# A double buffer for the exponents of an attention loop, turned in place, with the keys permuted as they are written

## The chip, the cores and the metric

The kernel runs on one core of a Trainium2 chip. The metric is the device time of one execution in microseconds. The kernel is written by hand for each engine: TensorE (PE) multiplies, VectorE (DVE) and ScalarE (ACT) work on its results, SyncE (SP) issues most DMAs and GpSimd (POOL) some. Engines wait for each other by semaphores that the code names. A matrix product in float32 stands in the trace as two instructions.

## The reference

Two layers of a mixed backbone over 256 context tokens and 1024 latent tokens. The change lies in the attention of each layer alone. The latent tokens attend to 512 cached keys and their own 1024, the context tokens to their own 256:

```python
s = jnp.einsum('bqhd,bkhd->bhqk', qi, k).astype(jnp.float32) * scale
p = jax.nn.softmax(s, axis=-1).astype(v.dtype)
return jnp.einsum('bhqk,bkhd->bqhd', p, v)
...
out = jnp.concatenate([attn_out, conv_out, cmlp_out], axis=-1) @ p['w_out']
```

After the projection each layer has an expert-choice feed-forward of 16 experts, which takes the larger part of the time.

## The kernel before

**Items.** Attention is cut into 18 items per layer (ITEMS, NI = 18). An item is one tile of 128 queries and a pair of heads ("slot" 0 and 1). Items 0 and 9 are the context ones (both query tiles, 256 keys each); the other 16 have 1536 keys, as 12 chunks of 128. The keys have no values of their own yet: probabilities are multiplied by the compressed context (CKVT), and value_heads expands the result afterwards.

**One item.** PE writes the scores of slot 0 to PSUM banks 0 to 2 and of slot 1 to banks 3 to 5 (scores, L1083, and the rotary part for both slots, rotary_scores, L1095). DVE takes the maximum of each slot over the 1536 keys (row_max, L1881, then L1885). ACT takes the exponents of a slot (exponents, L1539) into Pr[slot], a buffer per slot in r2. The next product needs keys on the partitions, so the exponents are transposed in two moves. DVE turns every 32x32 block (turn_blocks, L1893) from Pr[slot] to PB[slot], which lies in slot 1 of the ring; the same instruction permutes the blocks, since both of its access patterns are 4-dimensional with runs of 32 elements. Then SP issues 16 DMAs (exchange, L531), one for each pair of a destination quarter a and a source quarter b of the partitions: each moves 32 partitions x 2 runs of 384 floats into PTr[n % 2]. When all have landed (pt_landed[n % 2]), PE multiplies with the context (times_values, L1138; L1135 for the context items), in two halves of six chunks.

**Order.** Every engine runs its items in order. PE's iteration n is: scores of slot 0 of item n, the modulation matmuls of n-2 (L1109), first half of times_values(n-2), rotary scores of n, scores of slot 1, the transpose of the modulation, second half of times_values(n-2). DVE's is: bias_modulation(n-2), divide_out(n-3) (L1916), row_max of both slots, copy_modulation(n-2), turn_blocks of both slots, invert_sums (L1904). ACT's is: exponents of both slots, copy_out(n-2) (L1554). SP's is: load_ada (five DMAs: 2 MB of modulation weights, L516, and four small ones, L518) in items 0 to 7 of the first layer and 0 to 3 of the second, one of the two 2 MB units of W_OUT in each of the next two items, then the exchange. The modulation matmuls stand in PE's iterations 2 to 9 and 2 to 5. POOL sends the inverse sums through DRAM to all partitions (L717, L723), and DVE divides with them three items later.

**Waits around the change.** PB is a single buffer for both slots of one item. So turn_blocks(n) waits for pt_landed of item n-1: the DMAs must have read it. exponents(n) waits for p_turned of item n-1, and exchange(n) for p_turned of item n and, because of PTr, for o_summed of item n-2.

Of the kernel before, what the change touches and what calls it, by code (L numbers as in the profile page):

```python
# [20 lines left out]
PT = NP // P  # L21
# [24 lines left out]
ITEMS = []  # L46
# [11 lines left out]
def key_chunks(n):  # L58

    return 4 if ITEMS[n][1] is PROMPT_TILES else 12  # L60
# [48 lines left out]
def backbone(nc, x_prompt, x_sample, cache_ckv, cache_krope, c, c_ctx, w_ada, b_ada, norm1_g, norm2_g, w_in,  # L109
# [8 lines left out]
    with ExitStack() as ctx:  # L118
# [129 lines left out]
        Pr = [r2[:, 1536 * i:1536 * (i + 1)] for i in range(2)]  # L248
        PB = [ring[:, 1, 1536 * i:1536 * (i + 1)] for i in range(2)]
# [173 lines left out]
        def at(layer, per_layer, n):  # L423

            return layer * per_layer + n
# [17 lines left out]
        def _(sp):  # L443
# [21 lines left out]
            for l in range(DEPTH):  # L465
# [55 lines left out]
                def exchange(n):  # L521

                    x = key_chunks(n) * 32
                    sp.wait_ge(p_turned, at(l, 2 * NI, 2 * n + 2))
                    if n >= 2:
                        sp.wait_ge(o_summed, at(l, NI, n - 1))
                    for a in range(4):
                        for b in range(4):
                            dst = PTr[n % 2][32 * a:32 * a + 32, 0:8 * x].rearrange("p (s i x) -> p s i x", s=2, i=4)
                            src = ring[32 * b:32 * b + 32, 1, 0:3072].rearrange("p (s x) -> p s x", s=2)  # L530
                            sp.dma_start(dst[:, :, b, :], src[:, :, x * a:x * (a + 1)]).then_inc(pt_landed[n % 2], 16)  # L531

                for n in range(NI):
# [8 lines left out]
                    exchange(n)  # L542
# [12 lines left out]

                load_xd(0)
# [279 lines left out]
        def _(pe):  # L836
# [52 lines left out]
            for l in range(DEPTH):  # L889
# [230 lines left out]
                def times_values(n, chunks):  # L1120
# [8 lines left out]
                    rows = PTr[n % 2][:, 0:256 * key_chunks(n)].rearrange("p (s i x) -> p s i x", s=2, i=4)  # L1129
                    for c in chunks:  # L1130
                        if c >= key_chunks(n):
                            continue
                        moving = rows[:, :, :, 32 * c:32 * c + 32]
                        if t is PROMPT_TILES:
                            ins = pe.matmul(PS[:, 7, (c // 2) * 256:(c // 2 + 1) * 256], CKVT[:, c % 2, :], moving,  # L1135
                                            start=(c % 2 == 0), stop=(c % 2 == 1))
                        else:
                            ins = pe.matmul(PS[:, 7, 0:256], CKVT[:, PT + c, :], moving, start=(c == 0), stop=(c == 11))  # L1138
                        if c == key_chunks(n) - 1:
                            ins.then_inc(o_summed, 1)  # L1140
# [264 lines left out]
        def _(act):  # L1405
# [27 lines left out]
            for l in range(DEPTH):  # L1433
# [92 lines left out]

                def exponents(n, slot):
# [3 lines left out]
                    if n:  # L1531
                        act.wait_ge(p_turned, at(l, 2 * NI, 2 * (n - 1) + slot + 1))
                    if t is PROMPT_TILES:
                        for i in range(PT):
                            c = 2 * slot + i
                            ins = act.activation(Pr[slot][:, i * NP:(i + 1) * NP], psum(3 * slot + i, NP), ACT.Exp,
                                                 bias=nmax[:, c:c + 1], scale=SCALE, accum_out=psum_row[:, c:c + 1])
                    else:
                        ins = act.activation(Pr[slot], psum_wide(3 * slot, KEYS_S), ACT.Exp,  # L1539
# [166 lines left out]
        def _(dve):  # L1706
# [46 lines left out]
            for l in range(DEPTH):  # L1753
# [491 lines left out]
```

## Time and profile before

| | us |
|---|---|
| median of 3 runs | 2575.68 |
| lowest and highest | 2570.53, 2576.28 |
| the profiled execution | 2586.33 |
| its span from first to last instruction | 2584.6 |
| mean granted TensorE clock (share of full) | 0.957 |

Engine busy times of the profiled execution: PE 2363.8 us, DVE 746.5, ACT 509.5, POOL 277.1. The profiled execution is 10.7 us (0.4%) above the median, and 1.7 us of it lie outside its span. The chain that ended last is followed back from the last instruction: each piece of it is what released the next. "issue" in a chain is time for which the profile shows no wait. Sums of waits show how often one engine waited for another's work and how long in total.

### The profile page before, as it was taken

What the parts mean: (1) busy time and instruction counts of PE and PEld (TensorE: products, weight loads), DVE (VectorE), ACT (ScalarE), POOL (GpSimd) and SP (SyncE); (2) the same over time, 40 slices, a digit from 0 to 9 for tenths busy, and PEclk for the clock granted to TensorE, in tenths of its full rate; (3) what the DMA queues carried; (4) which work ended last, traced back from release to release, by engine and by line L of the source; (5) the groups of instructions that cost most, each with busy time, mean ns of one, the idle gap of its engine ahead of it and who ended that gap; (6) DMA issues with size and microseconds to landing.
All of it is one profiled execution on the core that took longest, in us unless ns stands there. A gap on an engine that the chain in (4) does not pass through costs nothing.

```text
span 2584.6 us, 30331 instructions
## 1 busy us (share of the span) xinstructions
PE 2363.8 (91%) x12256; PEld 1542.8 (60%) x12256; DVE 746.5 (29%) x1419; ACT 509.5 (20%) x1048; POOL 277.1 (11%) x434
## 2 busy tenths in 40 slices
PE   6999988778999899999999998877889959999996
PEld 4545545444445778878754455544444438888785
DVE  2302244444236211111142023434432371111113
ACT  3310222111234211101142002121113331101102
POOL 2000010101000121121210000210000001211211
PEclk8999999988999999999999999988899979999998
DMA  9000168755535788889940002864552248888888
GB/s 325 25 21 0 49 167 197 177 96 120 178 108 189 272 274 276 270 281 283 331 146 16 21 0 78 201 131 83 92 116 98 98 171 251 275 279 276 274 276 294
DMA packets 211770, 440.45 MB, mean 170 GB/s; under 512 B 23744, under 2 KB 71032, under 8 KB 211680
## 3 DMA queue, kind: packets, MB, share of 16 engines
q1 hardware_dynamic: 188912, 384.94, 48.0%
q0 software_dynamic: 22768, 54.29, 9.4%
q8 instruction: 59, 0.97, 0.2%
q14 instruction: 31, 0.25, 0.0%
HBM read 339.08 MB, written 47.65 MB: 150 GB/s over the span
## 4 chain that ended last, share of the span: by engine, by line
PE 68%; SPq 13%; DMA 9%; DVE 5%; issue 4%; ACT 1%; DVEq 0%; POOL 0%; POOLq 0%; ACTq 0%
SPq L531 13%; PE PS L1358 11%; PE PS L1365 11%; PE PS L1204 11%; PE PS L1390 8%; PE PS L990 8%; DMA r<-ring 6%; PE PS L944 5%; PE PS L931 5%; DVE ring L1893 2%; PE PS L1384 2%; PE PS L1044 1%; PE PS L1343 1%; PE PS L1216 1%; PE PS L898 1%
## 5 line engine op out<-in xcount | busy, mean ns | idle before, releaser
L1138 PE MATMUL PS<-r 128*128 128x256 f32 x768 | 220.9, 449 | 108.4 <-DMA r<-ring 108.4
L1358 PEld LDWEIGHTS PS<-r,ring 128*128 128x128 f32 x2048 | 281.5, 190 | 15.2 <-issue 15.2
L1204 PE MATMUL PS<-ring,mix 128*128 128x512 f32 x640 | 288.4, 598 | 1.2 <-DVE mix L1941 1.2
L1358 PE MATMUL PS<-r,ring 128*128 128x160 f32 x2048 | 283.6, 299 | 0.3 <-ACT r L1661 0.2
L1365 PE MATMUL PS<-r,ring 128*128 128x160 f32 x2048 | 283.4, 299 | 0.0
L1365 PEld LDWEIGHTS PS<-r,ring 128*128 128x128 f32 x2048 | 279.9, 190 | 0.0
L1138 PEld LDWEIGHTS PS<-r 128*128 128x128 f32 x768 | 171.4, 228 | 168.3 <-DMA r<-ring 128.8
L1390 PE MATMUL PS<-ring,r 128*128 128x512 f32 x496 | 221.1, 599 | 0.0
L990 PE MATMUL PS<-r,ring 128*128 128x512 f32 (+1 forms) x576 | 208.4, 521 | 1.6 <-ACT r L1482 1.6
L1083 PE MATMUL PS<-lat,r 128*128 128x512 f32 (+1 forms) x416 | 188.2, 587 | 10.2 <-ACT r L1539 5.4
L1204 PEld LDWEIGHTS PS<-ring,mix 128*128 128x128 f32 x640 | 116.4, 190 | 129.7 <-issue 129.7
L1539 ACT ACTIVATE r<-PS,nmax 128x1536 f32<-128x1536 f32 x64 | 98.6, 1541 | 461.6 <-DVE nmax L1885 461.6
L1893 DVE STREAM_TRANSPOSE ring<-r 128x1536 f32<-128x1536 f32 (+1 forms) x72 | 115.5, 1639 | 232.8 <-DMA r<-ring 232.1
L2153 DVE TENSOR_TENSOR r<-r,PS 128x320 f32<-128x320 f32 x64 | 31.2, 488 | 497.5 <-PE PS L1365 497.5
L990 PEld LDWEIGHTS PS<-r,ring 128*128 128x128 f32 x576 | 109.1, 190 | 100.6 <-issue 95.0
L1390 PEld LDWEIGHTS PS<-ring,r 128*128 128x128 f32 x496 | 91.7, 190 | 116.6 <-issue 116.6
L1881 DVE TENSOR_REDUCE pmax<-PS 128x1 f32<-128x1536 f32 x64 | 112.5, 1758 | 126.4 <-PE PS L1095 100.3
L944 PE MATMUL PS<-ring,r 128*128 128x512 f32 x320 | 140.0, 592 | 0.0
L1083 PEld LDWEIGHTS PS<-lat,r 128*128 128x128 f32 x416 | 75.2, 189 | 104.8 <-issue 86.8
L931 PE MATMUL PS<-ring,r 128*128 128x448 f32 x320 | 126.6, 550 | 0.0
L1672 ACT ACTIVATE r<-PS 128x320 f32<-128x320 f32 x64 | 24.5, 434 | 479.0 <-PE PS L1358 479.0
L1661 ACT ACTIVATE r<-PS,mod_all,scale_all 128x128 f32<-128x128 f32 x132 | 49.8, 456 | 277.5 <-PE PS L1343 277.5
(303 smaller groups left out, 2074.4 us busy)
## 6 DMA issues: line engine op xcount, KB each, us to landing
ring<-in_w_gate_dram SPq DMA_DIRECT2D x32, 2048.0 KB, 10.1
ring<-in_w_up_dram SPq DMA_DIRECT2D x32, 2048.0 KB, 11.6
ring<-in_w_down_dram SPq DMA_DIRECT2D x31, 2048.0 KB, 9.1
r<-ring SPq DMA_DIRECT2D x512, 96.0 KB, 4.5
ring<-in_w_ada_dram SPq DMA_DIRECT2D x15, 2048.0 KB, 10.1
x_dram<-r SPq DMA_DIRECT2D x20, 512.0 KB, 2.9
r<-x_dram SPq DMA_DIRECT2D x20, 512.0 KB, 4.2
mix<-in_w_ada_dram SPq DMA_DIRECT2D x4, 2048.0 KB, 15.0
```

The source lines that it names most:

```text
L531: sp.dma_start(dst[:, :, b, :], src[:, :, x * a:x * (a + 1)]).then_inc(pt_landed[n % 2], 16)
L931: ins = pe.matmul(psum(4 + t % 2, 448), hT[:, k, t * P:(t + 1) * P], W_IN[0][:, k, :], start=(k == 0), stop=(k == KD - 1))
L944: ins = pe.matmul(psum(t % 4, 512), hT[:, k, t * P:(t + 1) * P], W_IN[1][:, k, :], start=(k == 0), stop=(k == KD - 1))
L990: ins = pe.matmul(psum(base + j, tn), W_IN[u][:, k, c0:c0 + P], hT[:, k, t0:t0 + tn], start=(k == 0), stop=(k == KD - 1))
L1083: ins = pe.matmul(psum(3 * slot + c, w), QA[:, 2 * ITEMS[n][0] + slot, q], CKV[:, keys], start=(slot == 0), stop=(slot == 1))
L1138: ins = pe.matmul(PS[:, 7, 0:256], CKVT[:, PT + c, :], moving, start=(c == 0), stop=(c == 11))
L1204: ins = pe.matmul(psum(2 * (s % 2) + n, 512), mix[:, k, tile * P:(tile + 1) * P], W_OUT[n][:, k, :], start=(k == 0), stop=(k == KD - 1))
L1358: ins = pe.matmul(PS[:, b // 2, (b % 2) * 256:(b % 2) * 256 + SLOTS], W_G[:, k, b * P:(b + 1) * P], XST[par][:, k, :], start=(k == 0), sto ...
L1365: ins = pe.matmul(PS[:, 2 + b // 2, (b % 2) * 256:(b % 2) * 256 + SLOTS], W_U[:, k, b * P:(b + 1) * P], XST[par][:, k, :], start=(k == 0), ...
L1390: ins = pe.matmul(psum(4 + n, 512), HID[:, k, 0:CAP_S], w_down[:, k, n * 512:(n + 1) * 512], start=(k == 0), stop=(k == 3))
L1881: ins = dve.tensor_reduce(pmax[:, c:c + 1], psum_wide(3 * slot, KEYS_S), AX, ALU.max)
L1893: dve.transpose(PB[slot][:, 0:4 * x].rearrange("p (i c b) -> p c i b", i=4, b=32), Pr[slot][:, 0:4 * x].rearrange("p (c i a) -> p c i a", ...
```

## The change

It does five things, all in the attention loop.

1. Pr gets one buffer per item, for two items: the even items' exponents lie in r2[:, 0:3072], the odd ones' in ring slot 1, where PB was. PB is gone.
2. The exponents are written with the block permutation (by_chunk reads PSUM in key order, by_quarter writes quarter i of all chunks together, in runs of 32 floats).
3. The block transpose reads and writes the same contiguous range.
4. The exchange reads from Pr[n % 2]. For the 16 large items the pieces are the same as before (32 partitions x 2 runs of 384 floats). For the four context items a DMA has 4 runs of 64 floats, where it had 2 runs of 128.
5. The waits: exponents(n) waits for pt_landed of item n-2 (was p_turned of n-1); turn_blocks(n) no longer waits for pt_landed. Before the first tile of x is loaded behind the loop, SP waits for pt_landed[0], because that tile takes r2[:, 0:1024].

The context items' matmuls read their moving operand by another pattern, also in runs of 32 floats. The exchange takes its destination quarters as an argument, and the only call passes all four, in the same order as before, from SP.

```diff
-        Pr = [r2[:, 1536 * i:1536 * (i + 1)] for i in range(2)]
-        PB = [ring[:, 1, 1536 * i:1536 * (i + 1)] for i in range(2)]
+        Pr = [r2[:, 0:3072], ring[:, 1, 0:3072]]
...
-                def exchange(n):
-
-                    x = key_chunks(n) * 32
+                def exchange(n, quarters):
+
+                    groups, x = groups_of(n)
                     sp.wait_ge(p_turned, at(l, 2 * NI, 2 * n + 2))
                     if n >= 2:
                         sp.wait_ge(o_summed, at(l, NI, n - 1))
-                    for a in range(4):
+                    for a in quarters:
                         for b in range(4):
-                            dst = PTr[n % 2][32 * a:32 * a + 32, 0:8 * x].rearrange("p (s i x) -> p s i x", s=2, i=4)
-                            src = ring[32 * b:32 * b + 32, 1, 0:3072].rearrange("p (s x) -> p s x", s=2)
-                            sp.dma_start(dst[:, :, b, :], src[:, :, x * a:x * (a + 1)]).then_inc(pt_landed[n % 2], 16)
+                            dst = PTr[n % 2][32 * a:32 * a + 32, 0:4 * groups * x].rearrange("p (g x) -> p g x", g=groups)
+                            src = Pr[n % 2][32 * b:32 * b + 32, 0:4 * groups * x].rearrange("p (g x) -> p g x", g=groups)
+                            sp.dma_start(dst[:, :, x * b:x * (b + 1)], src[:, :, x * a:x * (a + 1)])\
+                                .then_inc(pt_landed[n % 2], 16)
...
+                sp.wait_ge(pt_landed[0], at(l, 256 * NI // 2, 256 * NI // 2))
                 load_xd(0)
...
                     act.wait_ge(max_ready, at(l, 2 * NI, 2 * n + slot + 1))
-                    if n:
-                        act.wait_ge(p_turned, at(l, 2 * NI, 2 * (n - 1) + slot + 1))
+                    if n >= 2:
+                        act.wait_ge(pt_landed[n % 2], at(l, 256 * NI // 2, 256 * (n // 2)))
...
-                        ins = act.activation(Pr[slot], psum_wide(3 * slot, KEYS_S), ACT.Exp,
+                        ins = act.activation(by_quarter(Pr[n % 2][:, slot * KEYS_S:(slot + 1) * KEYS_S]),
+                                             by_chunk(psum_wide(3 * slot, KEYS_S)), ACT.Exp,
...
-                    x = key_chunks(n) * 32
+                    groups, x = groups_of(n)
+                    w = 2 * groups * x
                     dve.wait_ge(exp_done, at(l, 2 * NI, 2 * n + slot + 1))
-                    if n:
-                        dve.wait_ge(pt_landed[(n - 1) % 2], at(l, 256 * NI // 2, 256 * ((n - 1) // 2 + 1)))
-                    dve.transpose(PB[slot][:, 0:4 * x].rearrange("p (i c b) -> p c i b", i=4, b=32),
-                                  Pr[slot][:, 0:4 * x].rearrange("p (c i a) -> p c i a", i=4, a=32)).then_inc(p_turned, 1)
+                    rows = Pr[n % 2][:, w * slot:w * (slot + 1)]
+                    dve.transpose(rows, rows).then_inc(p_turned, 1)
```

New functions that the diff calls:

```python
def groups_of(n):
    return (4, 64) if ITEMS[n][1] is PROMPT_TILES else (2, 384)
def by_chunk(keys):
    return keys.rearrange("p (c i a) -> p c i a", i=4, a=32)
def by_quarter(keys):
    return keys.rearrange("p (i c a) -> p c i a", i=4, a=32)
```

No instruction of the loop changes its place; its waits and buffers do. DVE in items 0 to 2 of the first layer before, from the transposes of item 0 to those of item 2 (L1881 and L1885 are the maxima, L1904 the inverse of the sums, L1954 and L1963 the modulation; "waits" names the semaphores):

```order
L1893 STREAM_TRANSPOSE ring<-r2 128x4x4x32 [waits exp_done] x2
L1904 RECIPROCAL oinv<-psum_row 128x4 [waits exp_done]
L1881 TENSOR_REDUCE pmax<-PS 128x1 [waits summed0]
L1885 TENSOR_SCALAR nmax<-pmax 128x1 [waits exp_done,dve_own]
L1881 TENSOR_REDUCE pmax<-PS 128x1 [waits summed1]
L1885 TENSOR_SCALAR nmax<-pmax 128x1 [waits exp_done,dve_own]
L1893 STREAM_TRANSPOSE ring<-r2 128x12x4x32 [waits pt_landed0,exp_done] x2
L1904 RECIPROCAL oinv<-psum_row 128x2 [waits exp_done]
L1954 TENSOR_TENSOR r1<-PS,r1 128x128 [waits ada_summed]
```

The same place now:

```order
L1905 STREAM_TRANSPOSE r2<-r2 128x512 [waits exp_done] x2
L1915 RECIPROCAL oinv<-psum_row 128x4 [waits exp_done]
L1893 TENSOR_REDUCE pmax<-PS 128x1 [waits summed0]
L1897 TENSOR_SCALAR nmax<-pmax 128x1 [waits exp_done,dve_own]
L1893 TENSOR_REDUCE pmax<-PS 128x1 [waits summed1]
L1897 TENSOR_SCALAR nmax<-pmax 128x1 [waits exp_done,dve_own]
L1905 STREAM_TRANSPOSE ring<-ring 128x1536 [waits exp_done] x2
L1915 RECIPROCAL oinv<-psum_row 128x2 [waits exp_done]
L1965 TENSOR_TENSOR r1<-PS,r1 128x128 [waits ada_summed]
```

The order is the same; the wait for pt_landed0 is gone from the transposes of item 1 (and its like from all later ones), and they work in place. ACT at the exponents of items 1 to 3 before (L1551 and L1554 are copy_out):

```order
L1539 ACTIVATE r2,psum_row<-PS,nmax 128x1536 [waits p_turned,max_ready] x4
L1551 ACTIVATE mix<-PS 128x2x256 [waits o_summed]
L1539 ACTIVATE r2,psum_row<-PS,nmax 128x1536 [waits p_turned,max_ready] x2
L1554 ACTIVATE mix<-PS 128x2x128 [waits o_summed]
L1539 ACTIVATE r2,psum_row<-PS,nmax 128x1536 [waits p_turned,max_ready] x2
```

The same place now:

```order
L1550 ACTIVATE ring,psum_row<-PS,nmax 128x12x4x32 [waits max_ready] x2
L1550 ACTIVATE r2,psum_row<-PS,nmax 128x12x4x32 [waits pt_landed0,max_ready] x2
L1563 ACTIVATE mix<-PS 128x2x256 [waits o_summed]
L1550 ACTIVATE ring,psum_row<-PS,nmax 128x12x4x32 [waits pt_landed1,max_ready] x2
L1566 ACTIVATE mix<-PS 128x2x128 [waits o_summed]
```

The exponents wait for the landing of the item two before, and write ring and r2 in turn.

## Rows read from the trace of the kernel before

**Rows 1.** The page, sections 1, 2 and 4: span, clock by slice, the chain's shares.

```profile
span 2584.6 us, 30331 instructions
...
PEclk8999999988999999999999999988899979999998
...
SPq L531 13%; PE PS L1358 11%; PE PS L1365 11%; PE PS L1204 11%; PE PS L1390 8%; PE PS L990 8%; DMA r<-ring 6%; PE PS L944 5%; PE PS L931 5%; DVE ring L1893 2%; PE PS L1384 2%; PE PS L1044 1%; PE PS L1343 1%; PE PS L1216 1%; PE PS L898 1%
```

**Rows 2.** Waits, 328 to 645 us: who <- for whom: us, times, longest.

```profile
DVE ring L1893 <- DMA r<-ring: 119.9, 17, 10.9
...
PE PS L1138 <- DMA r<-ring: 50.7, 15, 6.7
```

**Rows 3.** The chain in order of time, one item: start us, us, what.

```profile
537.75 4.84 DMA r<-ring
542.95 1.44 issue
544.39 1.75 DVE ring L1893
546.78 0.60 SPq L531
```

**Rows 4.** DVE in order of time, one item: start us, us, what [idle before].

```profile
528.03 0.12 DVE L1904 RECIPROCAL oinv<-psum_row 128x2 f32<-128x2 f32 x1
...
542.68 3.44 DVE L1893 STREAM_TRANSPOSE ring<-r 128x1536 f32<-128x1536 f32 x2 [6.12 <-DMA r<-ring]
...
552.87 0.15 DVE L1885 TENSOR_SCALAR nmax<-pmax 128x1 f32<-128x1 f32 x1
```

**Rows 5.** PE in order of time, an item without modulation matmuls.

```profile
542.63 2.86 PE L1138 MATMUL PS<-r 128*128 128x256 f32 x12 [2.89 <-DMA r<-ring]
545.42 2.85 PE L1095 MATMUL PS<-lat,r 64*128 64x512 f32 x12
548.20 2.84 PE L1083 MATMUL PS<-lat,r 128*128 128x512 f32 x6
550.88 2.75 PE L1138 MATMUL PS<-r 128*128 128x256 f32 x12
553.47 2.74 PE L1083 MATMUL PS<-lat,r 128*128 128x512 f32 x6
```

**Rows 6.** ACT in order of time, the same item.

```profile
550.29 1.54 ACT L1539 ACTIVATE r<-PS,nmax 128x1536 f32<-128x1536 f32 x1 [11.79 <-DVE nmax L1885]
...
553.06 1.54 ACT L1539 ACTIVATE r<-PS,nmax 128x1536 f32<-128x1536 f32 x1 [1.13 <-DVE nmax L1885]
554.50 0.19 ACT L1539 ACTIVATION_READ_ACCUMULATOR r<-PS,nmax 128x1 f32 x1
```

**Rows 7.** PE in order of time, an item with modulation matmuls.

```profile
384.32 2.85 PE L1095 MATMUL PS<-lat,r 64*128 64x512 f32 x12
...
395.15 1.95 PE L1109 MATMUL PS<-ring,r 128*32 128x128 f32 x64
398.84 2.86 PE L1138 MATMUL PS<-r 128*128 128x256 f32 x12 [1.74 <-DMA r<-ring]
```

**Rows 8.** SP in order of time: exchanges 0, 1 and 17 of layer 0, 0 and 17 of layer 1.

```profile
328.93 10.35 SPq L531 DMA_DIRECT2D r<-ring  x16
...
348.17 10.22 SPq L531 DMA_DIRECT2D r<-ring  x16
358.43 0.59 SPq L516 DMA_DIRECT2D ring<-in_w_ada_dram  x1
359.46 1.47 SPq L518 DMA_DIRECT2D r<-in_b_ada_dram  x4
...
639.30 10.82 SPq L531 DMA_DIRECT2D r<-ring  x16
...
1597.40 11.17 SPq L531 DMA_DIRECT2D r<-ring  x16
...
1907.57 10.72 SPq L531 DMA_DIRECT2D r<-ring  x16
```

**Rows 9.** PE in order of time, the start of layer 0's loop.

```profile
344.65 3.78 PE L1135 MATMUL PS<-r 128*128 128x256 f32 x8 [3.44 <-DMA r<-ring]
348.36 3.79 PE L1095 MATMUL PS<-lat,r 64*128 64x512 f32 x12
```

**Rows 10.** By stretch: us, engines' busy us, clock, DMA share, GB/s.

```profile
363.22:490.65 127.43, 106.95 (x720) 66.94 (x720) 54.27 (x82) 23.66 (x39) 20.62 (x38) 0.94 0.85 211
506.88:635.84 128.96, 100.35 (x321) 57.03 (x321) 53.66 (x57) 26.07 (x37) 12.55 (x21) 0.90 0.56 102
...
1762.80:1778.75 15.95, 15.59 (x49) 9.20 (x49) 5.50 (x9) 3.54 (x5) 1.31 (x2) 0.87 0.28 46
900.00:1200.00 300.00, 300.00 (x2033) 245.87 (x2033) 45.51 (x89) 32.70 (x72) 54.89 (x77) 1.00 0.88 276
```

**Rows 11.** Costliest groups of the page: out<-in xcount, busy, mean ns, idle before.

```profile
L1893 DVE STREAM_TRANSPOSE ring<-r 128x1536 f32<-128x1536 f32 (+1 forms) x72 | 115.5, 1639 | 232.8 <-DMA r<-ring 232.1
...
L1881 DVE TENSOR_REDUCE pmax<-PS 128x1 f32<-128x1536 f32 x64 | 112.5, 1758 | 126.4 <-PE PS L1095 100.3
```

**Rows 12.** POOL in order of time: the inverse sums of one item and the next.

```profile
528.71 0.71 POOL L717 DMA_DIRECT2D inv_dram<-oinv  x1 [9.40 <-DVE oinv L1904]
536.65 0.57 POOL L723 DMA_DIRECT2D lat<-inv_dram  x1 [7.23 <-DMA inv_dram<-oinv]
546.72 0.72 POOL L717 DMA_DIRECT2D inv_dram<-oinv  x1 [9.50 <-DVE mix L1916]
```

**Rows 13.** DMA issues: out<-in queue xcount, KB each, median us to landing.

```profile
lat<-inv_dram POOLq DMA_DIRECT2D x30, 128.0 KB, 4.9
```

More of the change, by code:

```diff
@@ L55, in parts_of @@
     return 2 if ITEMS[n][1] is PROMPT_TILES else 3
-def key_chunks(n):
-    return 4 if ITEMS[n][1] is PROMPT_TILES else 12
+def groups_of(n):
+    return (4, 64) if ITEMS[n][1] is PROMPT_TILES else (2, 384)
 UV_CHUNKS = [(1, 0), (1, 1), (0, 0), (0, 1), (2, 0), (2, 1), (0, 2), (0, 3), (1, 2), (1, 3), (2, 2), (2, 3)]
@@ L541, in _ @@
                         unit(0, (W_OUT[1], w_out_src[l, 1]))
-                    exchange(n)
+                    exchange(n, range(4))
                 def load_tail_chunk(c):
@@ L1128, in times_values @@
                             pe.wait_ge(o_copied, at(l, NI - 1, n))
-                    rows = PTr[n % 2][:, 0:256 * key_chunks(n)].rearrange("p (s i x) -> p s i x", s=2, i=4)
-                    for c in chunks:
[L1131 to L1139, printed above, removed]
+                    if t is PROMPT_TILES:
+                        rows = PTr[n % 2][:, 0:1024].rearrange("p (s t i c b) -> p t c s i b", s=2, t=PT, i=4, c=2)
+                        for c in chunks:
+                            if c < 4:
+                                ins = pe.matmul(PS[:, 7, (c // 2) * 256:(c // 2 + 1) * 256], CKVT[:, c % 2, :],
+                                                rows[:, c // 2, c % 2, :, :, :], start=(c % 2 == 0), stop=(c % 2 == 1))
+                            if c == 3:
+                                ins.then_inc(o_summed, 1)
+                        return
+                    rows = PTr[n % 2].rearrange("p (s i c b) -> p c s i b", s=2, i=4, c=12)
+                    for c in chunks:
+                        ins = pe.matmul(PS[:, 7, 0:256], CKVT[:, PT + c, :], rows[:, c, :, :, :], start=(c == 0), stop=(c == 11))
+                        if c == 11:
                             ins.then_inc(o_summed, 1)
@@ L1535, in exponents @@
                             c = 2 * slot + i
-                            ins = act.activation(Pr[slot][:, i * NP:(i + 1) * NP], psum(3 * slot + i, NP), ACT.Exp,
+                            ins = act.activation(by_quarter(Pr[n % 2][:, c * NP:(c + 1) * NP]), by_chunk(psum(3 * slot + i, NP)), ACT.Exp,
                                                  bias=nmax[:, c:c + 1], scale=SCALE, accum_out=psum_row[:, c:c + 1])
                     else:
-                        ins = act.activation(Pr[slot], psum_wide(3 * slot, KEYS_S), ACT.Exp,
+                        ins = act.activation(by_quarter(Pr[n % 2][:, slot * KEYS_S:(slot + 1) * KEYS_S]),
+                                             by_chunk(psum_wide(3 * slot, KEYS_S)), ACT.Exp,
                                              bias=nmax[:, 2 * slot:2 * slot + 1], scale=SCALE,
```

## The prediction

> **What bounds the kernel now.** I read the page first. The chain that ended last runs for 13% of its span through SP's issues of L531 and for 6% through the landing of their DMAs [rows 1], and both occur only in the attention loop. The waits of the first layer's loop say who pays: the block transposes wait 17 times for the exchange, 119.9 us, and times_values waits too, 50.7 us [rows 2]. The chain in order of time gives the loop's cycle: transpose, sixteen issues, last landing, and at once the next transpose, back to the first [rows 3]. In numbers: both transposes run from 542.68 to 546.12 [rows 4], issuing starts at 546.15, and from the end of a transpose to the last landing it is 528.1 (where L1904 begins, [rows 4]) to 542.6 (537.75 + 4.84, [rows 3]), 14.5 us. 14.5 + 3.5 = 18.0 us per item. The loop as a whole agrees: from exchange 0 to exchange 17 it is 639.30 - 328.93 = 310.4 us in the first layer and 1907.57 - 1597.40 = 310.2 in the second [rows 8], 18.25 each for 17 steps. No engine is full in that time. So the bound is one buffer: PB is written, sent, and only then written again.
>
> **The change, part by part.**
>
> *Two buffers for the exponents.* This removes the wait of 119.9 us per layer. What is late next? I follow one large item from the start R of its rotary scores, 545.42 [rows 5]. The second maximum is ready at 552.87 + 0.15 [rows 4], its exponents start at 553.06 and are read out at 554.69 [rows 6], so at R + 9.3. The second transpose needs half of 3.44 us [rows 4]; the first runs ahead of it, behind the maxima, which end at R + 7.6. SP can start at R + 11.2 (with 0.1 for hand-overs). The landing is 14.5 later, R + 25.7. Then comes the first half of times_values, 2.8 us [rows 5], and right behind it the rotary scores of the item two further. So two items take 11.2 + 14.5 + 2.8 = 28.5 us, if nothing else is slower: **14.2 us per item**.
>
> Other bounds per item: PE's own work. Without modulation it runs from 545.42 to 553.47 + 2.6 and has the first half of times_values besides, 10.7 + 2.8 = 13.5 us [rows 5]: hidden under 14.2, with 0.7 to spare. With modulation it is 384.32 to 397.10, plus 2.8, **15.6 us** [rows 7]: there PE is the bound. SP issues for 10.2 to 11.2 us [rows 8], plus 2.1 for the five DMAs of a modulation load (0.59 + 1.47, [rows 8]), and fits. In the seven steps of the second half of layer 0 DVE is busy for 53.7 us, 7.7 per item, and ACT for 26.1 [rows 10]. POOL stores at 528.71 and forwards at 536.65, 7.9 later; with 4.9 for the second landing its round is 13 us [rows 12, 13], and the result is wanted three items later. ACT's new wait, for landing n-2, costs nothing: exponents(n) start 4.9 us behind R (550.29 - 545.42, [rows 5, 6]), and landing n-2 has come before R, since PE's first half of times_values(n-2) waits for it; copy_out stands behind it on ACT and waits for PE anyway.
>
> The sum from exchange 0 to exchange 17. Start: unchanged up to the rotary scores of item 2, because they wait for exchange 0, which waited for nothing: 348.36 - 328.93 = 19.4 us [rows 8, 9]. Layer 0: 7 steps at 15.6 (up to item 9), 8 at 14.2, and 11.2 to exchange 17: 19.4 + 109.2 + 113.6 + 11.2 = 253.4; the context item 9 has a third of the scores, about -4: 249.4 against 310.4, **-61**. Layer 1: 3 steps at 15.6, 12 at 14.2: 19.4 + 46.8 + 170.4 + 11.2 = 247.8, about -2: 246 against 310.2, **-64**.
>
> *Exponents written permuted.* No row shows an exponent with runs of 32 floats. The nearest is the block transpose, whose two sides both had such runs: a large one took 1.75 us [rows 3] beside 1758 ns for a plain reduction of as many elements [rows 11]. I take 0. The other end is a doubling of the 1.54 us [rows 6]: both exponents then end at R + 11.3, 1 us more per item, about +32 us. A gain is excluded: the write is no shorter than before.
>
> *Transpose in place, contiguous.* 1.75 us against the 1.758 of the plain reduction [rows 3, 11]: nothing to gain, I take 0; 0.1 us either way would be 0.05 per item, 2 us.
>
> *The context items' exchange* has 256-byte runs where it had 512, twice as many. It counts four times, of which items 0 have no cover. The one stretch with only such an exchange had the DMA engines busy 0.28 x 15.95 = 4.5 us [rows 10]; twice that is 9 us, inside the 10.3 us of issuing [rows 8]: 0 to 1 us each. The upper end: a run costs as much as a 1536-byte one, of which half as many take 0.56 x 128.96 / 7 = 10.3 us [rows 10]; 20.6 us against 10.3 of issuing is 10 late, four times 40 us. I take 0, the nearer row. The Trainium skill, "DMA: Bandwidth & Descriptors", section "Specifications", speaks against this edit: below 512 B a transfer falls into read-modify-write. The same page, section "Why small descriptors are slow (HBM only)", exempts copies within SBUF. By the first rule an estimate would double the 9 us again, near the upper end; no run here yet shows which holds.
>
> *The loads that share the DMA engines.* With modulation loads they are busy 0.85 x 127.43 / 7 = 15.5 us per item, without them 10.3 [rows 10]. The demand stays, the step shrinks from 18.2 to 15.6: full. A landing may come later; PE's bound leaves 2 x 15.6 - 28.5 = 2.7 us per two items. I add 5 us in all.
>
> *SP's new wait* for pt_landed[0] stands behind exchange 17, some 14 us after exchange 16: nothing. If it were late, only the loads of x behind it would be.
>
> Behind the loop nothing is re-ordered, PE is bound by itself at clock 1.00 in the experts [rows 10], and every later stage starts behind PE: I count the whole gain. -61 - 64 + 5 = **-120 us**: 2586.3 becomes 2466. The median stands 10.7 below the profiled execution; I take the same difference from it: 2575.7 - 120 = **2456 us**.
>
> **Rivals.**
> - *The DMA engines become the bound where weights are loaded.* For it: 15.5 of 15.6 us. Against it: the experts' stage sustains 0.88 at 276 GB/s, and this would be no more than full. At 0.9 usable a step is 17.2, for 7 + 3 steps +16 us, and the two W_OUT loads of layer 1 and later landings some 10 more: 2482.
> - *Landings come early, PE alone bounds.* The gap was 14.5 with hardly any queue; if it falls by 1.4 or more, 20 steps shrink by 0.7: 2442.
> - *The permuted exponents or the short runs cost their upper ends.* 2456 + 32 = 2488, or + 40 = 2496.
> - *The wait only changes its place.* The landing is still on a cycle, now of two items. It decides when it takes as long as two old items: 11.2 + L + 2.8 > 36.5, L above 22.5 us where it is 14.5. If exchanges follow each other so closely that each waits for the one ahead in the queues, L could reach that, but then by throughput: 10.3 us of DMA work per item [rows 10] would have to be 18. At L = 24 a step is 19 us and the time 2575.7 + 34 x 0.75 = 2601: slower.
> - *It doesn't do what it says*: no gain if SP's queue were the bound, but SP is free for 18 - 10.8 us per item [rows 8]. 2576.
>
> **How the numbers follow.** Forecast (2445 to 2470): 0.62. DMA-bound loads (2482): 0.17. PE-bound (2442): 0.08. Costly writes (2488 to 2496): 0.07. No change: 0.02. Slower (2601): 0.04. The range from 2432 to 2500 holds the first four: 2432 is the PE-bound case with 10 us more of landings gained at the start of the loops, 2500 the costly write with half of the DMA-bound case. A measurement of this kernel tells 0.3% (8 us) from no change: faster by more 0.94, within 0.02, slower 0.04.
>
> **What would show it.** In the profile after: exchange 0 to exchange 17 in 250 and 246 us; the wait of the block transposes for the exchange gone; a wait of times_values for the exchange of about 0.7 us left in items without modulation and none with it; the clock of the loop near 1.00, since the gaps of 3 to 7 us are gone; L531 and the landing nearly out of the chain where there is modulation. An exponent above 1.6 us or a landing above 17 us would prove the sum wrong, and ACT waiting for the landing would prove the picture wrong.

## The result, and the profile after

The changed kernel takes 2511.06 us (median of 4, 2504.32 to 2514.92), the kernel before 2575.98: ratio 0.9742 [0.9707, 0.9777]. Run once more beside other kernels it gave 0.9753 [0.9721, 0.9786]. So 63 to 67 us are gone; 120 were forecast, and 2511 lies above the range. The profiled execution took 2512.68 us.

The page of the changed kernel: span, clock and DMA share by slice, the chain's shares by line (L530 is the exchange, L1141 times_values).

```profile
span 2510.9 us, 30259 instructions
...
PEclk8999999899999999999999999999999979999998
DMA  9000169867425788988950001985642258888888
...
PE PS L1361 11%; PE PS L1368 11%; PE PS L1207 11%; PE PS L1393 9%; PE PS L991 8%; SPq L530 7%; PE PS L945 5%; PE PS L932 5%; PE PS L1141 3%; DMA r<-r 3%; DMA r<-ring 2%; PE PS L1387 2%; PE PS L1084 2%; PE PS L1096 2%; PE PS L1045 1%; PE PS L1346 1%
```

SP's issues are at 7% where they had 13, the landings at 5 (two lines now, since the source is r2 or ring) where they had 6 [rows 1]. The transposes have left the list: the wait that was removed is gone. But the exchange is still on the chain for 12% of the span, some 300 us; where there is modulation it was to be nearly nothing.

SP in order of time, the changed kernel: start us, us, line.

```profile
329.28 10.41 SPq L530 DMA_DIRECT2D r<-r  x16
...
341.98 11.20 SPq L530 DMA_DIRECT2D r<-ring  x16
353.22 0.60 SPq L515 DMA_DIRECT2D ring<-in_w_ada_dram  x1
...
358.84 10.88 SPq L530 DMA_DIRECT2D r<-r  x16
...
461.24 11.33 SPq L530 DMA_DIRECT2D r<-r  x16
472.61 0.59 SPq L455 DMA_DIRECT2D ring<-in_w_out_dram  x1
476.92 17.39 SPq L530 DMA_DIRECT2D r<-ring  x16
505.33 10.22 SPq L530 DMA_DIRECT2D r<-r  x16
517.77 10.20 SPq L530 DMA_DIRECT2D r<-ring  x16
...
607.68 10.21 SPq L530 DMA_DIRECT2D r<-ring  x16
...
1571.07 11.12 SPq L530 DMA_DIRECT2D r<-r  x16
...
1835.85 11.42 SPq L530 DMA_DIRECT2D r<-ring  x16
```

From exchange 0 to 17 it is 607.68 - 329.28 = 278.4 us in layer 0 and 264.8 in layer 1, against 310.4 and 310.2 before [rows 8] and 249.4 and 246 in the sum. The rest of the execution, 2512.68 minus both loops, is 1969.5 us, and was 1965.7: the gain of the loops was kept behind them, as assumed.

PE in order of time, first halves of times_values that waited (L1134 is that of context item 0), and one that didn't:

```profile
344.17 3.60 PE L1134 MATMUL PS<-r 128*128 128x256 f32 x8 [2.60 <-DMA r<-r]
...
363.33 5.29 PE L1141 MATMUL PS<-r 128*128 128x256 f32 x12 [4.32 <-DMA r<-ring]
...
382.54 2.86 PE L1141 MATMUL PS<-r 128*128 128x256 f32 x12 [1.22 <-DMA r<-r]
...
430.47 2.86 PE L1141 MATMUL PS<-r 128*128 128x256 f32 x12
...
488.50 5.49 PE L1141 MATMUL PS<-r 128*128 128x256 f32 x12 [9.12 <-DMA r<-r]
...
520.63 5.15 PE L1141 MATMUL PS<-r 128*128 128x256 f32 x12 [4.56 <-DMA r<-r]
```

Read with the rows of SP, this gives the landings: exchange 1, issued from 341.98, is waited for until 363.33, 21.4 us; exchange 2 takes 358.84 to 382.54, 23.7; exchange 8 takes 461.24 to 488.50, 27.3. Exchange 10, with no 2 MB load near it, takes 505.33 to 520.63, 15.3. The semaphore events of the trace give the landings for which nobody waited too: exchanges 1 to 9 of layer 0 landed in 16.3 to 27.2 us, where the kernel before had 13.7 to 15.8 for the same nine. The chain in order of time shows where it sits: the last DMA of exchange 1 alone lands 10.78 us after its issue, that of exchange 3 after 9.08, where one took 4.84 [rows 3].

```profile
352.51 10.78 DMA r<-ring
363.29 0.04 issue
363.33 5.29 PE PS L1141 x12
...
390.35 9.08 DMA r<-ring
```

A load near by is not enough to make a landing late. Before, a W_OUT load went out 5.4 us ahead of exchange 8, which landed in 15.0 us; now it is 5.2 us ahead (456.09 and 461.24), and exchange 8 lands in 27.2. What differs is the exchange in front of it. Before, that one had always landed when the next was issued, since the single buffer made it so. Now exchange 7 landed at 467.6, 6.3 us behind the first issue of exchange 8. Over exchanges 1 to 8, the one with hardly any such overlap (exchange 5, 0.2 us) took least, 16.3 us, and the one with the most, exchange 8, took longest. Overlap alone does little: exchange 11, with 2.8 us of it and no load, landed in 14.2. The W_OUT loads are late too: 19.7 to 20.8 us to their own landing, before 8.2 to 10.9. So where an exchange, a load and the next exchange are under way at once, all of them take longer. This is a reading of one trace; no run separates the overlap from the load. The longest step, 28.4 us from exchange 9 to 10 with both W_OUT loads in front of it, is of this kind. Exchange 16 (20.1 us) has no load of SP beside it, but three of 512 KB that POOL issues.

By stretch, the kernel before (first fence) and the changed one: one stretch with 2 MB loads, one without. Columns as in [rows 10].

```profile
380.00:445.00 65.00, 57.68 (x389) 34.88 (x382) 30.23 (x41) 11.82 (x16) 4.60 (x7) 0.97 0.86 217
520.00:600.00 80.00, 63.33 (x202) 37.85 (x203) 34.52 (x36) 14.15 (x20) 5.13 (x8) 0.87 0.53 92
```

```profile
380.00:445.00 65.00, 62.42 (x475) 38.29 (x468) 32.14 (x46) 14.15 (x20) 7.36 (x13) 1.00 0.98 225
520.00:600.00 80.00, 76.05 (x266) 44.17 (x267) 38.81 (x41) 17.69 (x25) 7.16 (x11) 0.97 0.62 117
```

The DMA engines were busy for 0.86 of the stretch with loads and are for 0.98 now. In the stretch without loads they have room. ScalarE's new wait never shows: all its idle time before exponents ended with VectorE's maxima (207.3 and 187.8 us for the two buffers), none with a landing.

What was priced at nothing and cost nothing: the exponents written in runs of 32 floats, and the contiguous transpose in place.

```profile
L1550 ACT ACTIVATE ring<-PS,nmax x32: 1541/1541/1546, 335.2 to 1832.4; 128x1536 f32<-128x1536 f32 x32
...
L1905 DVE STREAM_TRANSPOSE ring<-ring x36: 706/1768/1779, 337.8 to 1834.0; 128x1536 f32<-128x1536 f32 x32, 128x512 f32<-128x512 f32 x4
```

1541 ns for the exponent as before [rows 6]; 1768 ns, median, for the transpose.

### The profile page after: what moved, and what is told of

The parts are those of the page before. It is cut to its first block, busy times and chain, and to the rows that moved or that the text cites. A ratio compares the mean times of both kernels' runs of the same rounds, so it can differ in the third digit from the quotient of the medians.

```text
span 2510.9 us, 30259 instructions
## 1 busy us (share of the span) xinstructions
PE 2336.3 (93%) x12256; PEld 1524.4 (61%) x12256; DVE 747.7 (30%) x1419; ACT 509.3 (20%) x1048; POOL 277.6 (11%) x434
## 4 chain that ended last, share of the span: by engine, by line
PE 78%; SPq 8%; DMA 6%; DVE 6%; issue 1%; ACT 1%; DVEq 0%; ACTq 0%
PE PS L1361 11%; PE PS L1368 11%; PE PS L1207 11%; PE PS L1393 9%; PE PS L991 8%; SPq L530 7%; PE PS L945 5%; PE PS L932 5%; PE PS L1141 3%; DMA r<-r 3%; DMA r<-ring 2%; PE PS L1387 2%; PE PS L1084 2%; PE PS L1096 2%; PE PS L1045 1%; PE PS L1346 1%
## 5 line engine op out<-in xcount | busy, mean ns | idle before, releaser
L1141 PE MATMUL PS<-r 128*128 128x256 f32 x768 | 198.8, 414 | 62.4 <-DMA r<-r 32.1
L1141 PEld LDWEIGHTS PS<-r 128*128 128x128 f32 x768 | 156.5, 208 | 114.4 <-DMA r<-r 41.0
L1084 PE MATMUL PS<-lat,r 128*128 128x512 f32 (+1 forms) x416 | 188.2, 587 | 10.2 <-ACT ring L1550 3.8
L1393 PEld LDWEIGHTS PS<-ring,r 128*128 128x128 f32 x496 | 91.7, 190 | 116.6 <-issue 116.6
L945 PEld LDWEIGHTS PS<-ring,r 128*128 128x128 f32 x320 | 59.6, 190 | 68.9 <-issue 68.9
L2182 DVE SCALAR_TENSOR_TENSOR r<-PS,gate_s,r 128x1024 f32<-128x1024 f32 x31 | 39.8, 1284 | 199.8 <-PE PS L1393 199.8
```

The costliest lines, as they stand in the source:

```text
L945: ins = pe.matmul(psum(t % 4, 512), hT[:, k, t * P:(t + 1) * P], W_IN[1][:, k, :], start=(k == 0), stop=(k == KD - 1))
L1084: ins = pe.matmul(psum(3 * slot + c, w), QA[:, 2 * ITEMS[n][0] + slot, q], CKV[:, keys], start=(slot == 0), stop=(slot == 1))
L1141: ins = pe.matmul(PS[:, 7, 0:256], CKVT[:, PT + c, :], rows[:, c, :, :, :], start=(c == 0), stop=(c == 11))
L1393: ins = pe.matmul(psum(4 + n, 512), HID[:, k, 0:CAP_S], w_down[:, k, n * 512:(n + 1) * 512], start=(k == 0), stop=(k == 3))
```

## The experiments

Ratios are to the kernel before on the same chip. "Loops" are the times from exchange 0 to exchange 17 in layers 0 and 1 of the profiled execution, read as the ends of the last transpose of items 0 and 17.

| run | ratio [95%] | loops, us |
|---|---|---|
| changed kernel | 0.9742 [0.9707, 0.9777] | 278.4, 264.8 |
| the same again | 0.9753 [0.9721, 0.9786] | 275.2, 267.4 |
| one old wait back (waitback) | 1.0005 [0.9988, 1.0023] | 310.1, 301.2 |
| light loads (light) | 0.9586 [0.9564, 0.9609] | 259.0, 255.5 |
| light loads again (light_again) | 0.9594 [0.9577, 0.9612] | 248.1, 248.0 |
| kernel before, light loads (before_light) | 0.9967 [0.9955, 0.9980] | 314.2, 306.8 |
| 512-byte runs (r512) | 0.9751 [0.9733, 0.9770] | 291.3, 277.0 |
| light loads, 512-byte runs (light512) | 0.9559 [0.9543, 0.9575] | 255.0, 250.0 |
| loads sent later (late) | 0.9731 [0.9689, 0.9773] | 271.1, 259.4 |
| exchange split over SP and ACT (actsplit) | 0.9546 [0.9511, 0.9581] | 248.4, 237.7 |
| kernel before, split (before_split) | 0.9669 [0.9644, 0.9694] | 263.3, 258.4 |
| split and 512-byte runs (split512) | 0.9531 [0.9504, 0.9558] | 261.7, 240.6 |
| split and light loads (light_split) | 0.9434 [0.9415, 0.9454] | 235.5, 234.1 |
| split and loads later (late_act) | 0.9683 [0.9617, 0.9749] | 255.2, 258.3 |
| light loads, waits filled (light_fill) | 0.9601 [0.9585, 0.9617] | 250.5, 252.7 |

light, before_light, r512 and light512 ran on a chip on which the kernel before takes 2592 us; on the others it takes 2576 to 2578. Their ratios can be compared with the others, their loops only with each other.

**The wait, and nothing else: waitback.**

```diff
                     dve.wait_ge(exp_done, at(l, 2 * NI, 2 * n + slot + 1))
+                    if n:
+                        dve.wait_ge(pt_landed[(n - 1) % 2], at(l, 256 * NI // 2, 256 * ((n - 1) // 2 + 1)))
                     rows = Pr[n % 2][:, w * slot:w * (slot + 1)]
```

> The changed kernel with one wait of the kernel before put back: the block transposes of an item wait again until the exchange of the item before has landed. Layout, buffers, permuted exponents, transposes in place and 256-byte runs stay changed. If the second buffer is the whole gain, the time goes back to the kernel before, ratio 0.995 to 1.002, the rest being what the new layout costs or gives. If permuting where the keys are written or turning in place gave part of the 65 us, the ratio stays below 0.99.

Ratio 1.0005. With the old wait the whole gain is gone: the second buffer is all of it, and the permuted write, the transposes in place and the other layout give nothing by themselves, within 0.2%. A small cost of theirs could hide behind the old wait here; that they have none in the changed kernel rests on the 1541 and 1768 ns above.

**The loads: light and before_light.**

```diff
-                    sp.dma_start(ada_w[i % 2], ada_src[la, n]).then_inc(ada_landed[i % 2], 16)
+                    sp.dma_start(ada_w[i % 2][:, 7:8, :], ada_src[la, n][:, 7:8, :]).then_inc(ada_landed[i % 2], 16)
...
-                        unit(2, (W_OUT[0], w_out_src[l, 0]))
+                        unit(2, (W_OUT[0][:, 0:1, :], w_out_src[l, 0][:, 0:1, :]))
...
-                        unit(0, (W_OUT[1], w_out_src[l, 1]))
+                        unit(0, (W_OUT[1][:, 0:1, :], w_out_src[l, 1][:, 0:1, :]))
```

> The changed kernel, but each 2 MB load inside the attention loop (12 modulation units and 4 of W_OUT) moves only 256 KB of it; the rest of these weights is whatever lies there, so this part of the result is left wrong. Number of DMAs, of matmuls and all waits are the same. Theory L (the bulk loads share the DMA engines with the exchange, and its landing stretches from 14.5 us to 17 to 27 us behind the first issue): the loops come down from 278 and 265 us, exchange 0 to exchange 17, to what the prediction's sum gave, 250 and 246, and the time to about 2511 - 45 = 2466 us. Theory C (the 256-byte runs of the context items alone): the loops with loads keep their steps, and less than 10 us go, 2503 us. Theory P (POOL's round of inverse sums, which also became longer, holds up VectorE): POOL's stores speed up without loads too, so the time falls as with L, but VectorE would then have waited for POOL's landings in the changed kernel, and its trace shows no such wait.

> The kernel before with the same light loads (256 KB of each 2 MB; those weights are wrong). It tells whether the loads cost anything when the loop is held by the single buffer. Theory L: next to nothing in layer 0, since the load was sent behind an exchange and had landed before the next one was issued 8 us later: steps of 18.0 instead of 18.2 us, time down by 2 to 10 us. If it fell by 40 us like the changed kernel, the loads would have been as costly before and my reading of a new collision would be wrong.

Light loads (256 KB in place of 2 MB, so part of the weights is missing) bring the changed kernel to 0.9586, and later to 0.9594, against 0.9742 and 0.9753: 1.6% or 41 us. The kernel before gains 0.3%, 8 us, from the same edit. So the same bytes on the same path cost some 33 us more since the loop is tighter. The stretch of above, with light loads:

```profile
380.00:445.00 65.00, 65.00 (x460) 39.19 (x459) 34.05 (x48) 14.73 (x21) 5.33 (x9) 1.00 0.72 126
```

PE is busy for all 65 us of it, at full clock, and its steps are 15.5 us: its own bound. The loops of the second run with light loads begin and end here (SP; exchanges 8 and 11 of layer 0 between):

```profile
329.22 10.40 SPq L530 DMA_DIRECT2D r<-r  x16
...
447.98 10.21 SPq L530 DMA_DIRECT2D r<-r  x16
...
491.17 10.22 SPq L530 DMA_DIRECT2D r<-ring  x16
...
577.29 10.26 SPq L530 DMA_DIRECT2D r<-ring  x16
...
1542.93 11.13 SPq L530 DMA_DIRECT2D r<-r  x16
...
1790.93 9.32 SPq L530 DMA_DIRECT2D r<-ring  x13
```

577.29 - 329.22 = 248.1 and 1790.93 - 1542.93 = 248.0 us. The sum of the prediction, without its 5 us for the loads, had 249.4 and 246. The first run with light loads, on another chip, had 259.0 and 255.5, so the agreement to 1 or 2 us is luck and to 5% is not. In layer 0 the 30.3 us between this run and the changed kernel lie in three parts: 13.2 up to exchange 8 (132.0 against 118.8), 13.3 in the three steps from there to exchange 11, where the W_OUT loads and context item 9 are (56.5 against 43.2), and 3.8 behind it. POOL is ruled out as the holder of the loop: in the changed kernel its stores took up to 13.6 us, but no wait of VectorE for its landings is in the trace.

**The short runs: r512 and light512.** The context item's exponents are written by quarter, query tile and chunk, so that a quarter is one run of 128 floats per slot.

```diff
-    return (4, 64) if ITEMS[n][1] is PROMPT_TILES else (2, 384)
+    return (2, 128) if ITEMS[n][1] is PROMPT_TILES else (2, 384)
...
+                            out = Pr[n % 2][:, slot * 512:(slot + 1) * 512].rearrange("p (i t c a) -> p t c i a", i=4, t=2, a=32)[:, i, :, :, :]
```

> The changed kernel with the context items' exponents in another order within a slot (quarter, query tile, chunk), so that their exchange has 512-byte runs as before; all else the same. Theory C: context item 9 of each layer had a landing of up to 28 us and 19 us behind its first issue, where the kernel before had 15; the short runs account for 5 to 12 us per layer, time 2490 to 2500. Theory L: these landings are late because of the W_OUT load, the four context exchanges save at most 2 us each: 2505 to 2511.

> Both edits at once (light loads, part of the weights wrong, and 512-byte runs). If the two causes are all there is, the loops take 246 to 250 us and the time is 2460 to 2466; if they overlap, no less than with light loads alone. Anything still missing against 2456 would be a third cause, such as the clock or POOL.

r512 has the ratio of the changed kernel. With light loads the 512-byte runs are 0.27% faster (0.9559 against 0.9586 on the same chip, intervals that overlap), some 7 us that may be none. In r512, exchanges 8 and 9 of layer 0 landed in 28.7 and 22.9 us, so short runs are not what made them late. The context exchange of item 0, which meets no load, landed 344.17 - 329.28 = 14.9 us behind its first issue, before 344.65 - 328.93 = 15.7 [rows 8, 9]. The time sees no price of the short runs, but the DMA engines do. The stretch in which SP issues exchange 0 of layer 0, in the kernel before, the changed one and r512:

```profile
328.93:339.27 10.34, 9.40 (x29) 3.39 (x27) 3.85 (x5) 3.26 (x4) 1.32 (x2) 1.00 0.20 45
```

```profile
329.28:339.69 10.41, 9.47 (x31) 3.46 (x33) 5.65 (x7) 3.26 (x4) 1.32 (x2) 1.00 0.30 44
```

```profile
329.15:339.50 10.35, 9.41 (x29) 3.39 (x27) 5.59 (x7) 3.26 (x4) 1.32 (x2) 1.00 0.21 45
```

For the same bytes the engines' share is 0.30 with 256-byte runs and 0.20 or 0.21 with 512-byte ones; in layer 1 it is 0.55 against 0.20 and 0.24. It stays hidden because issuing takes 10.4 us anyway. The Trainium skill, "DMA: Bandwidth & Descriptors", says in "Specifications" that below 512 B a transfer falls into read-modify-write; its section "Why small descriptors are slow (HBM only)" exempts copies within SBUF from the price of small transfers. These shares do not bear the exemption out as far as the engines' work goes; whether read-modify-write is the reason, no run here shows.

**The order of the loads: late.**

```diff
                 for n in range(NI):
+                    if n and n < len(ADA_ITEMS[l]) + 2:
+                        sp.wait_ge(p_turned, at(l, 2 * NI, 2 * n + 1))
                     if n < len(ADA_ITEMS[l]):
                         load_ada(n)
```

> The changed kernel with each 2 MB load of the loop (from item 1 on) sent later: not right behind the last DMA of the exchange before it, but after the first transpose of its own item, some 2 us before the next exchange. The same bytes, the same DMAs. Theory B (the load right behind an exchange delays that exchange's last DMAs, whose landing took 9 to 16 us in the steps with loads): the landings return to 15 to 17 us and 15 to 30 us of the time go, ratio 0.963 to 0.969. Theory L (the 16 DMA engines are simply full there, share 0.96 to 1.06 in the steps from 396 to 488 us): the order does not matter, ratio 0.971 to 0.977 as the changed kernel has.

0.9731: no difference that these intervals can tell. That the load stands right behind the exchange is not the trouble. Sent later, it still meets one: exchanges 1 and 2 of layer 0 landed in 21.7 and 23.0 us.

**The issuing: actsplit, before_split, light_split, split512, late_act.** ScalarE issues the quarters 2 and 3, SyncE 0 and 1.

```diff
-                    exchange(n, range(4))
+                    exchange(n, range(2))
...
+                def exchange(n, quarters):
+
+                    groups, x = groups_of(n)
+                    act.wait_ge(p_turned, at(l, 2 * NI, 2 * n + 2))
+                    for a in quarters:
+                        for b in range(4):
...
+                            act.dma_start(dst[:, :, x * b:x * (b + 1)], src[:, :, x * a:x * (a + 1)])\
+                                .then_inc(pt_landed[n % 2], 16)
...
                     copy_out(n - 2)
+                    exchange(n, range(2, 4))
```

> The changed kernel with the destination quarters 2 and 3 of every exchange issued by ScalarE, behind its copy_out, and 0 and 1 by SyncE: 8 issues of 0.64 us each side by side, not 16 in a row. Theory S (where no load runs, the landing is held by SyncE's 10.2 us of issuing): it lands 10 us behind the second transpose, not 14.5 to 17, TensorE is the bound at 13.5 us per item where it now is 14.2 to 15.4, and the low clock behind its waits goes too: 20 to 35 us less, ratio 0.960 to 0.966. Theory T (it is held by the engines' own 10.3 us of work): landing at 13 or more, at most 8 us less.

0.9546, 117 us below the kernel before and some 53 below the changed one: more than expected. SP and ScalarE in order of time and a stretch with loads of this kernel:

```profile
522.82 6.40 SPq L530 DMA_DIRECT2D r<-ring  x8
...
522.82 6.64 ACTq L1577 DMA_DIRECT2D r<-ring  x8
...
529.89 1.54 ACT L1550 ACTIVATE r<-PS,nmax 128x1536 f32<-128x1536 f32 x1 [8.64 <-DVE nmax L1909]
```

```profile
380.00:445.00 65.00, 65.00 (x465) 39.11 (x462) 33.04 (x47) 14.14 (x20) 7.65 (x14) 1.00 1.02 245
```

ScalarE's eight issues end at 529.46, just before the next exponents. Side by side an issue takes 0.80 to 0.83 us, where SP alone needs 0.64 (10.2 for 16): issuing falls from 10.2 us to 6.6, not to half. And in the stretch with loads the DMA engines are as full as in the changed kernel, 1.02 against 0.98 (a share can exceed 1, as this view counts), while PE is busy for all 65 us. My expectation, which gave the split an effect only where no load runs, was wrong, and with it the plain form of theory L. Full engines don't set the step by themselves. What counts is the landing against what two steps leave for it, 2 x 15.6 - 14.0 = 17.2 us: an exchange that takes 10 to 11 us to issue and then 9 to 11 to land its last DMA misses that, one that takes 6 to issue doesn't, in most steps. In layer 0 of this run exchanges 1 to 9 landed in 13.5 to 17.5 us.

> The kernel before, with one buffer for the turned blocks and all its waits, but destination quarters 2 and 3 of every exchange issued by ScalarE. Its cycle is two transposes and the landing. If the landing is 9.5 to 10 us behind them where no load runs (theory S), the step is 13 to 13.6 us there and 15.6 to 18 with loads, the time 2576 - 90 = about 2485, ratio 0.955 to 0.970: the issuing would then be worth more than the second buffer. If the landing is held by the DMA engines (theory T), the step is above 16 us and the ratio 0.985 or more.

The same split in the kernel before gives 0.9669: more than the second buffer, 0.9748 on average. Its steps, read from the starts of the rotary scores, are 13.3 to 14.6 us in layer 0's last five and 15.6 to 17.1 with loads, behind a first one of 19.7. Theory S holds: issuing, 10.2 of 18.0 us, was the greater part of the cycle that the prediction read as one of buffers.

> Split exchange and light loads (256 KB of each 2 MB of the loop; those weights are wrong). TensorE is the bound in every step then: exchange 0 to 17 in 240 and 232 us or less, time 2577 x 0.950 = 2448. If the loads still cost something with two issuing queues, this is more than 10 us faster than the split alone; if the shorter landing has hidden their effect, less than 8.

0.9434, 0.0112 or 29 us below the split with full loads. So the loads still cost with two issuing engines. In this run nearly every step, by the starts of the rotary scores, is at PE's own 15.5 us with modulation and 12.3 to 14.2 elsewhere; it shows the floor of this structure.

> The changed kernel with the split exchange and with 512-byte runs in the context items. The split alone gave 0.9546 [0.9511, 0.9581]. Theory C: its one long step, 17.0 us in front of item 10 in the first layer, where the context exchange and a W_OUT load meet, falls to 14: 2 to 5 us, ratio 0.952 to 0.955. Otherwise the same ratio.

0.9531 [0.9504, 0.9558] is not told apart from 0.9546 [0.9511, 0.9581]. Its long step in layer 0 was not shortened: 18.0 us, where the split alone had 17.0.

Split exchange and loads sent later together (late_act):

> Both edits together. If B and S both hold, all steps come near TensorE's own 15.6 and 13.5 us: 40 to 60 us less than the changed kernel, ratio 0.950 to 0.958. If L holds, the steps with loads stay at 16 to 17 us and the ratio is that of the split alone, 0.960 to 0.966.

0.9683: with both queues busy, sending the load late is clearly worse than not (0.9546), though its four times fall in two pairs, 2476 and 2506. SP and then the chain in one of its long steps:

```profile
1627.18 0.40 SPq L455 DMA_DIRECT2D ring<-in_w_out_dram  x1
...
1634.62 17.07 DMA r<-ring
1651.73 5.49 PE PS L1143 x12
```

The last DMA of that exchange landed 17 us after its issue. The load had been sent at 1627.18, 1.7 us ahead of the exchange's first issue, and I read it as still in the engines' way. Why the times fall in two pairs stays open.

**The low clock: light_again and light_fill.** TensorE behind its longest wait in the changed kernel, first half of times_values for item 8:

```profile
488.50:494.00 5.50, 5.50 (x14) 3.95 (x14) 0.00 (x0) 0.00 (x0) 4.35 (x9) 0.50 0.65 165
```

The granted clock is 0.50, the 1.2 GHz level, behind 9.1 us of waiting, and the matmuls take 5.49 us where they take 2.86 at 1.00. light_fill adds this to light:

```diff
+                    if chunks[0] == 0 and n % 2 == 0 and 8 <= n < NI - 2:
+                        pe.wait_ge(ada_copied, ADA_AT[l] + len(ADA_ITEMS[l]))
+                        for _ in range(5):
+                            pe.matmul(PS[:, 6, 256:512], ident[:, :], CKVT[:, 0:2, :], start=True, stop=True)
```

> The kernel with light loads once more (256 KB of each 2 MB of the loop; those weights are wrong), as a reference on this chip: ratio 0.956 to 0.961.

> Light loads, and in front of the first half of times_values of the even items from 8 to 14, where TensorE waits 2 to 5 us for the exchange, five matmuls of 256 columns into an unused part of PSUM bank 6, some 2.1 us of work with no use. Nothing else changes. Theory K (the wait leaves TensorE at 1.2 GHz, so the six matmuls behind it take 4.3 to 5.5 us instead of 2.8, and since the second buffer this lies on the cycle): with the wait filled they take 2.8 to 3.5 us, the long steps shrink by 1 to 2 us, eight of them per kernel: 5 to 12 us less than with light loads alone. Otherwise the filling costs 0 to 8 us, because it delays the matmuls where the exchange has already landed.

PE in order of time with filled waits (L1129 is the filling):

```profile
521.12 2.32 PE L1129 MATMUL PS<-r,ident 128*128 128x256 f32 x10
...
549.88 2.32 PE L1129 MATMUL PS<-r,ident 128*128 128x256 f32 x10
553.10 2.86 PE L1145 MATMUL PS<-r 128*128 128x256 f32 x12 [0.90 <-DMA r<-r]
```

Here the matmuls behind the filled wait take 2.86 us, but the whole gives 0.9601 against 0.9594: no gain. In layer 0 of the reference only one of the four filled items (item 8, 5.35 us) had met the low clock; in the other three the matmuls took 2.86 us without filling, as with it. So the run hardly tests theory K. The low clock behind long waits is real in the changed kernel (5.29, 5.49 and 5.15 us above), but what it costs of the time no run shows.

## Why the prediction was wrong, point by point

**Right: the bound, and that it would go.** The single buffer's wait held the loop; waitback shows it to 0.2%. The gain stayed a gain behind the loop.

**Right: PE's own steps.** 15.6 us with modulation: the rotary scores in layer 0 start at 417.76 and 433.25, 15.5 apart. Without loads 14.2 were forecast; the last seven steps of the loops took 102.3 and 101.5 us, 14.6 and 14.5 each.

**Right: the edits priced at nothing.** Exponents, transposes, the new waits of ScalarE and SP, and within some 7 us the short runs, though these do take more of the DMA engines.

**Wrong, the failed step: "The loads that share the DMA engines".** The prediction saw 15.5 us of DMA work against a step of 15.6, gave the landing 2.7 us of slack per two items, and added 5 us. The landings took 6.9 to 12.8 us longer than the 14.5 of the sum (21.4, 23.7, 27.3), not under 2.7, and both loops together took 543 us, not 500: 43 us. The prediction took 14.5 us as a constant, read where an exchange never overlapped the one before it, and removed the wait that kept them apart. Its own sign of a wrong sum, a landing above 17 us, came true. Light loads take 41 us off the time, some 33 of them the change's own, since the kernel before also gains 8; there the same loads made no landing late (13.7 to 15.8 us).

**The rivals.** DMA-bound steps of 17.2 us (2482) had the place right and the size wrong: it let the step stretch by the engines' total work, not by the landing. "The wait only changes its place" was nearer to the mechanism: landings that stretch because exchanges follow each other closely. It set the limit at 22.5 us, and exchanges 2, 7, 8 and 9 of layer 0 passed it (23.7, 22.9, 27.2 and 24.6). It took this for all 34 steps and so came out slower than no change (2601, given 0.04); in fact it came only where loads run.

**Wrong in a second, smaller term: the median.** The profiled execution of before was 10.7 us above its median, and the prediction took the whole gain from both. But that excess seems to have lain in the loops: outside them the kernel before takes 1965.7 us, and waitback, profiled at 2577.5, takes 1966.2 there and 611.3 in the loops, not 620.6. What the sum computed was the time with the loops made new, so by this comparison of two profiles some 9 us of the 120 were never in the median.

**What is left.** 120 were forecast and 65 came. 43 us in the loops, 9 of the median and 4 outside the loops make the 55. The loads cost 41 us, and the sum had 5 for them, so they explain some 36 of the 43, give or take the 8 us that the intervals of the ratios leave open. The rest may be landings above 14.5 us without loads (15.3 for exchange 10) and the low clock behind them; the runs don't divide these, and the loops with light loads differ by more between two chips (514 and 496 us).

**Not seen at all: the cheaper half of the cycle.** The sum had 10.2 us of issuing in the 14.5 and treated it as given. Splitting it over two engines is worth 3.3% to the kernel before, which keeps its single buffer, and 2.1% more to the changed one. The split version at 0.9546 beats both kernels.

## What to carry to other kernels

Removing a buffer's wait makes transfers meet that used to take turns. Before counting its gain, compare the landing, not the engines' total work, with the time that the new cycle leaves for it. A landing read where transfers took turns is no constant: ask whether the next exchange will be issued before this one has landed, and whether a bulk load falls between them. Look first at how long the issuing itself takes: where many small DMAs of one engine stand in the cycle, a second issuing engine shortens it without any buffer. And when a profiled execution is above the median, find out where before subtracting.

## What the runs showed of the hardware

- Beside 2 MB loads, and with the exchange before not yet landed, the last 96 KB DMA of an exchange landed up to 16.5 us after its issue (exchange 8, by its semaphore events), where it took 4.8 [rows 3]; with two issuing engines and the load just ahead it took 17. A W_OUT load's own landing went from 8.2 to 10.9 us to 19.7 to 20.8.
- With the exchanges kept apart, loads sent 5 to 8 us ahead of them made no landing late (13.7 to 15.8 us).
- Eight DMAs issued by ScalarE took 6.64 us while SyncE took 6.40 for its eight; SyncE alone needs 10.2 for sixteen. Both together filled the same DMA engines (share 1.02, 245 GB/s) without holding up TensorE in that stretch.
- Copies within SBUF in runs of 256 bytes landed no later than in runs of 512 (14.9 and 15.7 us for the same 16 DMAs), held by their issuing, but kept the DMA engines busy for 0.30 and 0.55 of the stretch, not 0.20 to 0.24.
- The DMA share of a stretch with loads was 0.98 where TensorE waited and 1.02 where it didn't: a full share alone doesn't say what a step takes.
